# Scaling the attention probabilities of three groups of heads on ScalarE instead of VectorE, in a four-layer single-core kernel

## The chip, the cores and the metric

The kernel is one program on one core of a Trainium2 chip. Its engines are TensorE (PE in the profile), VectorE (DVE), ScalarE (ACT), GpSimd (POOL, idle here) and SyncE (SP, which issues the DMAs). The metric is the device time of one execution in microseconds (us). Every engine works through its own instructions in order; a wait at the head of an engine's queue holds all that is behind it.

## The reference

Two kinds of layer, two layers of each, on 256 tokens of width 1024. The first kind is not touched. The second kind projects its input to four attention mixers of four heads each, and the change is in the softmax of three of them:

```
def forgetting_attention(q, k, v, log_f):            # mixer b
    ...
    logits = einsum('bthd,bshd->bhts', qb, k) * scale
    logits = where(causal, logits + decay, NEG_INF)
    probs = softmax(logits, axis=-1)
    return einsum('bhts,bshd->bthd', probs, v)
# dsa_attention (mixer a): the same with the keys cut to the top-k of an index score
# sliding_window_sink_attention (mixer d): the same with a window, and a sink in the sum
# differential_attention (mixer c): probs[:, 0] - lam * probs[:, 1], of 8 maps
x = x + rmsnorm(mix @ w_out); m = square(relu(h @ w_up)) @ w_down; ...
```

## The kernel before

All matmuls are on TensorE, most of them with operands split into a rounded high part and a remainder, three matmuls for one product. A weight panel goes by DMA into a ring of 8 slots; ScalarE writes its rounded part (`round_weights`, L2575) and VectorE the remainder (`subtract_rounded`, L2757, signal `panels_subtracted`) before TensorE may use it.

A layer of the second kind begins with the mixers. Each engine has there an order written out by hand, the table `ORDER`: a list of words such as `in` (one projection), `panel` (one weight panel), `c`, `b`, `a`, `d` (one step of that mixer). Each engine's part of a mixer is a generator (`attend`, `attend_d`), and each word runs it to its next `yield`. The mixers come in the order c, b, a, d. The 256 queries of a mixer are two tiles, t=0 (128 keys) and t=1 (256 keys). For mixer i and tile t the steps are:

- TensorE `scores`: the logits into PSUM banks (`name_sc..`).
- VectorE `masked_scores` (L2819, L2823, L2828): scale, mask and move them to the buffer `Ls[i % 2]`, row maxima, signal `score_max`.
- ScalarE `exps` (L2587): one exponential for each head with the negative maximum as bias and the row sum as second output (`den`), signal `exps`.
- VectorE `probs`: reciprocal of the sums (L2843), one multiplication of all heads by it (L2845: 128x512 for t=0, 128x1024 for t=1), signal `probs`. For c two more instructions (L2849) subtract the second map.
- TensorE `turned` (L2240): transposes of the probabilities; ScalarE `turned_rows_of` moves them out of PSUM (`drain_bank`, L2579, written to `all_rest`), signal `PT`; TensorE `values`.

After its values, mixer c has a norm: ScalarE copies `c_o` out of PSUM and squares it (L2652, signal `o_sq`), TensorE sums the squares (`c_ss`, a 128x512 product behind the wait on `o_sq`), ScalarE makes the reciprocal root (L2656, L2658), VectorE applies it (L2950). In ScalarE's order this copy and square stand right behind the exponentials of b, t=1. The parts `early`, `rest` and `late` on TensorE are the output projection `mix`; `early` waits until VectorE has split the results of c and b (L2763, L2765, signal `mix_split`).

The name `all_work` in the profile holds the buffers of scores, q, k and v and many others, `all_rest` the transposed probabilities, `all_ring` the weight panels. Numbers of lines in both files differ by a few.

Of the kernel before, what the change touches and what calls it, by code (L numbers as in the profile page):

```python
# [11 lines left out]
ALU = mybir.AluOpType  # L12
ACT = mybir.ActivationFunctionType
# [4 lines left out]
NT = T // P  # L18
# [100 lines left out]
class Signals:  # L119
# [11 lines left out]
    def due(self, layer, name, n):  # L131
        return self.sem[name], self.base[name] + layer * self.per_layer[name] + n
# [82 lines left out]
class Memory:  # L215
# [9 lines left out]
    def area(self, name):  # L225
        return Area(self.plain[name][:, :], self.parts[name])
# [64 lines left out]
def turns_in(order, steps, size=lambda step: 1):  # L291

    at = {key: [i for i, x in enumerate(order) if x == name][step] for key, (name, step) in steps.items()}
    return {key: sum(size(other) for other in at if at[other] <= at[key]) for key in at}
# [400 lines left out]
def params2(a):  # L695
# [27 lines left out]
    return out  # L723

SIGNALS2 = {
    "raw": 9, "copied": 6, "roped": 9, "probs": 8, "PT": 12, "o_sq": 1, "nlf": 1, "mix_split": 5, "gT": 16, "p_split": 1, "score_max": 8, "exps": 8,
    "gate_abs": 9, "gate_ln": 1, "relu_used": 6, "relu": 6, "c_oT": 1, "o_rstd": 1, "lam_sum": 1, "lam_exp": 1, "pT_in": 1, "ff_relu": 16,
    "ff_squared": 16, "g_hi": 16, "gates": 4, "cosined": 9, "proj_out": 4, "o_copied": 2,
}


# [1385 lines left out]
def block2(nc, ctx, kit, banks, ring_all, A, earlier):  # L2117

    rounded, hT, mixT, x = kit.rounded, kit.hT, kit.mixT, kit.x
    S = Signals(nc, ctx, SIGNALS2, earlier)  # L2120
# [4 lines left out]
    def psum_of(layer):  # L2125
        return banks.of(f"2{layer}")

    def ring_of(layer):
        return ring_all.of(f"2{layer}")

    def due_in(layer):
        return lambda name, n: S.due(layer, name, n)
# [22 lines left out]
    lam = buf(80)  # L2155
# [9 lines left out]
    raw, turned = area(2, 2, T), area(2, 2, T)  # L2165
    LN = 8 * P * 3
    Ls = [area(LN), area(LN)]
# [11 lines left out]
    gates, proj, yn = area(4, 512), area(4, 512), area(4, 512)  # L2179

    def scores_of(buffer, t, maps):

        n = P * (t + 1)
        lo = maps * P * t
        return buffer[:, lo:lo + maps * n].rearrange("p (e n) -> p e n", n=n)
# [19 lines left out]
    ATTENDED = [("c", 8, 32 ** -0.5, 4), ("b", 4, HD ** -0.5, 2), ("a", 4, HD ** -0.5, 0), ("d", 4, HD ** -0.5, 6)]  # L2205
# [16 lines left out]
            a:3 split:2 d in d:2 panel d early p early d a early rest early d:2 rest late rest late d rest"""),  # L2222
    }
    MIXERS = [(name, t) for name, *_ in ATTENDED for t in range(NT)]
    maxima, probabilities, exponentials = (turns_in(ORDER[engine], {(name, t): (name, first + t) for name, t in MIXERS})
                                           for engine, first in (("DVE", 0), ("DVE", 2), ("ACT", 1)))
    turned_rows = turns_in(ORDER["ACT"], {(name, t): (name, 3 if name == "d" and not t else 4 + t) for name, t in MIXERS}, lambda step: step[1] + 1)
    copied_out = turns_in(ORDER["ACT"], {"b": ("b", 6), "a": ("a", 6)})
    split_off = turns_in(ORDER["DVE"], {"c": ("split", 0), "b": ("split", 1), "a": ("split", 2), "d0": ("d", 5), "d1": ("d", 7)})
# [4 lines left out]
    def tensor(pe, layer, following):  # L2234

        psum, ring, due = psum_of(layer), ring_of(layer), due_in(layer)
        mm, mm3, used = kit.mm, kit.mm3, kit.used

        def transpose(out, a):
            return nc.tensor.transpose(out, a, kit.ident)  # L2240
# [110 lines left out]
        def turned(i, t):  # L2351

            name, maps, _, _ = ATTENDED[i]
            pe.wait_ge(*due("probs", probabilities[name, t]))
            for kt in range(t + 1):
                b = psum.claim(pe, f"{name}_pt{t}{kt}")
                for e in range(4):
                    m = e if maps == 4 else 4 * (e // 2) + e % 2
                    last = transpose(b[:, e * P:(e + 1) * P], scores_of(Ls[i % 2], t, maps)[:, m, kt * P:(kt + 1) * P])
                last.then_inc(psum.full_of(f"{name}_pt{t}{kt}"), 1)  # L2360
# [199 lines left out]
    def stat_of(i, t, what, n):  # L2560

        lo = 16 + 48 * (i % 2) + 8 * t + {"neg": 0, "den": 16, "rec": 32, "sink": 36}[what]
        return stat[:, lo:lo + n]

    def scalar(act, layer):

        psum, ring, due = psum_of(layer), ring_of(layer), due_in(layer)
        A_ = nc.scalar.activation
# [8 lines left out]
        def drain_bank(name, out, signal, rows=slice(0, P), part=slice(0, 512)):  # L2577
            act.wait_ge(*psum.filled(name))
            A_(out, psum.bank(name)[rows, part], ACT.Copy).then_inc(*psum.freed(name))  # L2579
            act.drain().then_inc(S[signal], 1)  # L2580

        def exps(i, t):
            name, maps, _, _ = ATTENDED[i]
            act.wait_ge(*due("score_max", maxima[name, t]))
            L = scores_of(Ls[i % 2], t, maps)
            for e in range(maps):
                A_(L[:, e, :], L[:, e, :], ACT.Exp, bias=stat_of(i, t, "neg", maps)[:, e:e + 1],  # L2587
                   accum_out=stat_of(i, t, "den", maps)[:, e:e + 1])
            if name == "d":
                A_(stat_of(i, t, "sink", 4), stat_of(i, t, "sink", 4), ACT.Exp)  # L2590
            act.drain().then_inc(S["exps"], 1)

        def project():

            yield
            for name, panel, kind, parts in IN_USES:
                if name in ROPED_AT:
                    i = ROPED_AT[name]
                    tiles = ROPED[i][3]
                    if i >= 2:  # L2600
                        act.wait_ge(*due("roped", i - 1))
                    drain_bank(name, raw[:, i % 2, 0:tiles, :], "raw", part=slice(0, tiles * T))
                elif name in ("b_q", "b_k"):
                    drain_bank(name, qk[name], "copied")
                elif name in vtok:
                    drain_bank(name, vtok[name], "copied", part=slice(0, NT * parts[1]))
                yield
            yield
# [24 lines left out]
        def turned_rows_of(i, t):  # L2633
            name = ATTENDED[i][0]
            if i >= 2 and not t:
                act.wait_ge(*psum.filled(ATTENDED[i - 2][0] + "_o"))
            for kt in range(t + 1):
                drain_bank(f"{name}_pt{t}{kt}", PTs[i % 2][:, kt, :, t * P:(t + 1) * P], "PT")

        def attend(i):  # L2640
            name = ATTENDED[i][0]
            yield
            for t in range(NT):
                exps(i, t)
                yield
            yield
            for t in range(NT):
                turned_rows_of(i, t)
                yield
            if name == "c":  # L2650
                drain_bank("c_o", oT, "c_oT")
                A_(osq, oT, ACT.Square).then_inc(S["o_sq"], 1)  # L2652
                yield
                kit.exp_and_ln()
                act.wait_ge(*psum.filled("c_ss"))
                A_(ors, shaped(psum.bank("c_ss"), 2, T), ACT.Ln, bias=kit.eps, scale=1.0 / HD).then_inc(*psum.freed("c_ss"))  # L2656
                act.drain()
                A_(ors, ors, ACT.Exp, scale=-0.5).then_inc(S["o_rstd"], 1)  # L2658
                yield
                yield  # L2660
            else:
                drain_bank(name + "_o", qk[name + "_q"], "o_copied")
                yield
            yield

        def attend_d():
            yield
            for t in range(NT):
                exps(3, t)
                yield  # L2670
            turned_rows_of(3, 0)
            yield
            yield
            turned_rows_of(3, 1)
            yield
            yield
            yield
# [69 lines left out]
    def vector(dve, layer):  # L2747

        psum, ring, due = psum_of(layer), ring_of(layer), due_in(layer)
        PAR = par_of(layer)  # L2750
        V = nc.vector
# [82 lines left out]
        def probs(i, t):  # L2834
            name, maps, _, _ = ATTENDED[i]
            n = P * (t + 1)
            L = scores_of(Ls[i % 2], t, maps)
            den, rec = stat_of(i, t, "den", maps), stat_of(i, t, "rec", maps)
            dve.wait_ge(*due("exps", exponentials[name, t]))
            if name == "d":  # L2840
                V.tensor_tensor(den, den, stat_of(i, t, "sink", 4), ALU.add)
                dve.drain()
            V.reciprocal(rec, den)  # L2843
            dve.drain()
            V.tensor_tensor(L, L, rec.unsqueeze(2).broadcast_to([P, maps, n]), ALU.mult)  # L2845
            if name == "c":
                dve.drain()
                for g in range(2):
                    V.scalar_tensor_tensor(L[:, 4 * g:4 * g + 2, :], L[:, 4 * g + 2:4 * g + 4, :], lam[:, 68:69],  # L2849
                                           L[:, 4 * g:4 * g + 2, :], ALU.mult, ALU.add)  # L2850
            dve.drain().then_inc(S["probs"], 1)

        def select(t):
# [407 lines left out]
```

## Time and profile before

| | |
|---|---|
| median of 3 runs | 1681.28 us (1680.44 to 1684.38) |
| profiled execution, its own time | 1682.12 us |
| its span | 1680.3 us |
| mean granted TensorE clock | 0.977 of full |
| PE busy | 1594.1 us (95%) |
| DVE busy | 1093.7 us (65%) |
| ACT busy | 767.5 us (46%) |

The profile is of one execution. The two layers of the second kind take the last half of the span; their mixer parts lie around 900 to 1055 us and 1320 to 1450 us. Busy shares are means over parts with different limits; what matters for an edit in the mixers is which wait ends last there.

### The profile page before, as it was taken

To read this page: it belongs to the slowest core of one execution; us is meant where nothing else is said; L and a number is where in the kernel's file an instruction comes from. 1 tells how busy PE (TensorE), PEld (TensorE's weight loads), DVE (VectorE), ACT (ScalarE), POOL (GpSimd) and SP (SyncE) were. 2 spreads that over 40 slices of the span, in tenths; PEclk is the share of its full clock that TensorE was granted. 3 is DMA by queue.
4 is the path that set the end of the run, shared out by engine and by line. 5 is a ranking of instruction groups with operands and counts; after the bars stand their busy time and mean duration, and the time that the engine had idled before them with its cause. 6 is when DMAs were issued, how large, how long until landed. Compare 5 with 4: busy or idle time off the path is not lost.

```text
span 1680.3 us, 29569 instructions
## 1 busy us (share of the span) xinstructions
PE 1594.1 (95%) x12124; PEld 1425.4 (85%) x12124; DVE 1093.7 (65%) x1609; ACT 767.5 (46%) x1151; POOL 0.2 (0%) x4
## 2 busy tenths in 40 slices
PE   7999989999999989899999989999999979999998
PEld 7987569998898856799989877899889978799887
DVE  2865666776466666577854897666353798766545
ACT  3524254444345332544443355655344446655434
POOL 0000000000000000000000000000000000000000
PEclk9999899999999989899999999999999989999999
DMA  7421024655642200366554432456554433355552
GB/s 249 145 87 52 1 80 138 193 175 201 198 138 69 77 26 1 125 216 199 190 201 121 122 80 92 159 176 201 190 197 134 127 92 109 103 189 198 186 190 100
DMA packets 186310, 232.23 MB, mean 138 GB/s; under 512 B 22560, under 2 KB 161600, under 8 KB 186048
## 3 DMA queue, kind: packets, MB, share of 16 engines
q1 hardware_dynamic: 186176, 230.34, 42.5%
q8 instruction: 96, 1.57, 0.4%
q14 instruction: 38, 0.31, 0.1%
HBM read 229.28 MB, written 1.05 MB: 137 GB/s over the span
## 4 chain that ended last, share of the span: by engine, by line
PE 83%; DVE 10%; DVEq 3%; issue 2%; ACT 2%; DMA 1%; ACTq 0%; SPq 0%
PE banks L432 82%; DVE all_ring_rounded L2757 2%; DVE all_rest L2926 1%; DVE all_work L2861 1%; DMA all_ring<-in_w_ple_gate 1%; DVEq L2860 1%; DVE x_state L381 0%; DVE all_work L2823 0%; PE banks L2240 0%; DVEq L384 0%; DVE all_work L2819 0%; DVE all_work L2845 0%; ACT all_rest L2579 0%; DVEq L2821 0%; PE banks L927 0%
## 5 line engine op out<-in xcount | busy, mean ns | idle before, releaser
L432 PE MATMUL banks<-all_mix_rounded,all_ring_rounded 128*128 128x256 f32 (+2 forms) x3584 | 666.7, 287 | 17.0 <-DVEq L428 7.5
L432 PEld LDWEIGHTS banks<-all_mix_rounded,all_ring_rounded 128*128 128x128 f32 (+2 forms) x3584 | 566.5, 193 | 26.6 <-DVEq L428 8.7
L432 PE MATMUL banks<-all_work_rounded,all_ring_rounded 128*128 128x256 f32 x1792 | 511.1, 285 | 0.0
L432 PE MATMUL banks<-all_ring_rounded,all_work_rounded 128*128 128x512 f32 (+1 forms) x1856 | 462.4, 377 | 3.2 <-DVE all_ring_rounded L2757 1.7
L432 PEld LDWEIGHTS banks<-all_ring_rounded,all_work_rounded 128*128 128x128 f32 x1856 | 347.0, 188 | 69.6 <-issue 2.7
L432 PEld LDWEIGHTS banks<-all_work_rounded,all_ring_rounded 128*128 128x128 f32 x1792 | 346.1, 193 | 1.8 <-issue 1.4
L2757 DVE TENSOR_TENSOR all_ring_rounded<-all_ring,all_ring_rounded 128x2048 fp32r<-128x2048 f32 x104 | 237.6, 2291 | 149.6 <-ACT all_ring_rounded L2575 146.8
L1609 DVE TENSOR_TENSOR all_ring_rounded<-all_ring,all_ring_rounded 128x2048 fp32r<-128x2048 f32 (+2 forms) x96 | 213.6, 2232 | 83.3 <-ACT all_ring_rounded L1366 80.8
L2575 ACT ACTIVATE all_ring_rounded<-all_ring 128x2048 fp32r<-128x2048 f32 x104 | 198.2, 1910 | 118.9 <-DMA all_ring<-in_w_mlp_down 87.1
L1366 ACT ACTIVATE all_ring_rounded<-all_ring 128x2048 fp32r<-128x2048 f32 (+2 forms) x96 | 177.7, 1858 | 112.4 <-DMA all_ring<-in_w_in 54.3
L432 PE MATMUL banks<-all_work 64*64 64x64 f32 (+10 forms) x2084 | 172.9, 272 | 18.5 <-ACTq L1541 6.0
L432 PEld LDWEIGHTS banks<-all_work 64*64 64x64 f32 (+4 forms) x2084 | 124.3, 153 | 47.6 <-issue 24.8
L432 PE MATMUL banks<-all_ring_rounded,all_mix_rounded 128*128 128x256 f32 (+2 forms) x640 | 143.7, 307 | 3.3 <-DVE all_ring_rounded L2757 2.3
L432 PEld LDWEIGHTS banks<-all_ring_rounded,all_mix_rounded 128*128 128x128 f32 x640 | 103.8, 191 | 11.9 <-DVE all_ring_rounded L2757 2.8
L432 PE MATMUL banks<-all_work,all_ring 128*128 128x128 f32 x704 | 101.7, 289 | 1.9 <-issue 1.9
L432 PEld LDWEIGHTS banks<-all_work,all_ring 128*128 128x128 f32 x704 | 87.9, 195 | 3.0 <-issue 3.0
L1583 ACT ACTIVATE all_work<-all_work 128x256 f32<-128x256 f32 x44 | 18.4, 418 | 125.3 <-DVE all_work L2017 125.3
L1370 ACT ACTIVATE all_work<-banks 128x512 f32<-128x512 f32 (+2 forms) x74 | 37.1, 502 | 81.9 <-PE banks L432 65.8
L432 PEld LDWEIGHTS banks<-all_rest,all_work 128*64 128x64 f32 (+2 forms) x504 | 48.4, 164 | 22.7 <-issue 9.0
L432 PE MATMUL banks<-all_rest,all_work 128*128 128x128 f32 (+5 forms) x504 | 60.6, 289 | 6.9 <-ACTq L2580 5.0
L432 PE MATMUL banks<-all_work,all_rest 128*64 128x256 f32 (+7 forms) x292 | 58.6, 379 | 2.4 <-ACT all_work L1377 2.1
L2715 ACT ACTIVATE all_work<-banks 128x512 f32<-128x512 f32 x32 | 19.1, 597 | 81.8 <-PE banks L432 81.8
(258 smaller groups left out, 1252.8 us busy)
## 6 DMA issues: line engine op xcount, KB each, us to landing
all_ring<-in_w_in SPq DMA_DIRECT2D x48, 1024.0 KB, 5.4
all_ring<-in_w_mlp_up SPq DMA_DIRECT2D x32, 1024.0 KB, 5.4
all_ring<-in_w_mlp_down SPq DMA_DIRECT2D x32, 1024.0 KB, 4.9
all_ring<-in_ffn_w_gate SPq DMA_DIRECT2D x22, 1024.0 KB, 5.3
all_ring<-in_ffn_w_up SPq DMA_DIRECT2D x22, 1024.0 KB, 5.5
all_ring<-in_ffn_w_down SPq DMA_DIRECT2D x22, 1024.0 KB, 4.9
all_ring<-in_w_out SPq DMA_DIRECT2D x16, 512.0 KB, 4.3
all_ring<-in_w_out SPq DMA_DIRECT2D x8, 1024.0 KB, 5.0
```

Of the source, the lines that this page charges most:

```text
L432: ins = self.nc.tensor.matmul(out, lhsT, rhs, start=start, stop=stop)
L1366: A_(rounded(ring.view(name + "_hi")), raw, ACT.Copy).then_inc(ring_all.rounded, 1)
L1370: A_(out, psum.bank(name)[rows, part], func, scale=scale).then_inc(*psum.freed(name))
L1583: A_(gcv[:, j % 2, 2, :], gcv[:, j % 2, 1, :], ACT.Gelu_apprx_tanh).then_inc(S["ff_gelu"], 1)
L1609: V.tensor_tensor(rounded(ring.view(name)), ring.view(name), as_float32(rounded(ring.view(name + "_hi"))), ALU.subtract).then_inc(ring_all ...
L2575: A_(rounded(ring.view(name + "_hi")), raw, ACT.Copy).then_inc(ring_all.rounded, 1)
L2715: A_(gh[:, 2 * c:2 * c + 2, :], shaped(psum.bank(f"ff{c}"), 2, T), ACT.Relu).then_inc(*psum.freed(f"ff{c}"))
L2757: V.tensor_tensor(rounded(ring.view(name)), ring.view(name), as_float32(rounded(ring.view(name + "_hi"))), ALU.subtract).then_inc(ring_all ...
L2860: dve.drain()
L2861: V.max(best, acc[t])
L2926: last = V.scalar_tensor_tensor(acc[t], r, weight, acc[t], ALU.mult, ALU.add)
```

## The change

For b, a and d VectorE's `probs` stops after the reciprocal and raises a new signal, `inverted`. ScalarE gets a new function, `scale_probs`: it waits for `inverted` and multiplies each head's scores, with a Copy activation whose scale is the column of reciprocals, in four instructions of 128x128 (t=0) or 128x256 (t=1), then raises `scaled`, for which TensorE's transposes now wait. Mixer c is as before. `scale_probs(i, 0)` runs in the same step as the exponentials of t=1, `scale_probs(i, 1)` in the next step; `ORDER` is not changed.

```
         def turned(i, t):
...
-            pe.wait_ge(*due("probs", probabilities[name, t]))
+            pe.wait_ge(*(due("probs", t + 1) if name == "c" else due("scaled", scaled[name, t])))
...
+        def scale_probs(i, t):
+            name, maps, _, _ = ATTENDED[i]
+            act.wait_ge(*due("inverted", inverted[name, t]))
+            L = scores_of(Ls[i % 2], t, maps)
+            for e in range(maps):
+                A_(L[:, e, :], L[:, e, :], ACT.Copy, scale=stat_of(i, t, "rec", maps)[:, e:e + 1])
+            act.drain().then_inc(S["scaled"], 1)
...
             for t in range(NT):
                 exps(i, t)
-                yield
+                if t and name != "c":
+                    scale_probs(i, 0)
+                yield
+            if name != "c":
+                scale_probs(i, 1)
             yield
...
         def attend_d():
             yield
-            for t in range(NT):
-                exps(3, t)
-                yield
+            exps(3, 0)
+            yield
+            exps(3, 1)
+            scale_probs(3, 0)
+            yield
+            scale_probs(3, 1)
             turned_rows_of(3, 0)
...
             V.reciprocal(rec, den)
+            if name != "c":
+                dve.drain().then_inc(S["inverted"], 1)
+                return
             dve.drain()
             V.tensor_tensor(L, L, rec.unsqueeze(2).broadcast_to([P, maps, n]), ALU.mult)
```

Three places of the order show what moves. The first is ScalarE in the first layer of the second kind, from the exponentials of b, t=1 on (`bank2` is the projection b_v, `bank0` is `c_o`, and the line after them is the square). Before:

```order
L2587 ACTIVATE all_work<-all_work 128x256 [waits score_max]
L2587 ACTIVATE all_work<-all_work 128x256 x3
L2579 ACTIVATE all_work<-banks 128x512 [waits bank2_filled]
L2579 ACTIVATE all_work<-banks 128x512 [waits bank0_filled]
L2652 ACTIVATE all_work<-all_work 128x512
L2575 ACTIVATE all_ring_rounded<-all_ring 128x2048 [waits slot3_freed,slot2_filled]
L2579 ACTIVATE all_work<-banks 128x512 [waits bank1_filled]
L322 ACT_TABLE_LOAD
```

And of the change, at the same place:

```order
L2590 ACTIVATE all_work<-all_work 128x256 [waits score_max]
L2590 ACTIVATE all_work<-all_work 128x256 x3
L2601 ACTIVATE all_work<-all_work 128x128 [waits inverted]
L2601 ACTIVATE all_work<-all_work 128x128 x3
L2582 ACTIVATE all_work<-banks 128x512 [waits bank2_filled]
L2582 ACTIVATE all_work<-banks 128x512 [waits bank0_filled]
L2667 ACTIVATE all_work<-all_work 128x512
L2578 ACTIVATE all_ring_rounded<-all_ring 128x2048 [waits slot3_freed,slot2_filled]
L2582 ACTIVATE all_work<-banks 128x512 [waits bank1_filled]
L2601 ACTIVATE all_work<-all_work 128x256 [waits inverted]
L2601 ACTIVATE all_work<-all_work 128x256 x3
L322 ACT_TABLE_LOAD
```

The two copies and the square of c now stand behind four instructions that wait for VectorE. The second place is VectorE at the reciprocals that this waits for, those of b. Before:

```order
L2757 TENSOR_TENSOR all_ring_rounded<-all_ring,all_ring_rounded 128x2048 [waits panels_rounded] x2
L2843 RECIPROCAL all_work<-all_work 128x4 [waits exps]
L2845 TENSOR_TENSOR all_work<-all_work 128x512
L2843 RECIPROCAL all_work<-all_work 128x4 [waits exps]
L2845 TENSOR_TENSOR all_work<-all_work 128x1024
L2950 SCALAR_TENSOR_TENSOR all_work<-all_work 128x512 [waits o_rstd]
```

And of the change:

```order
L2775 TENSOR_TENSOR all_ring_rounded<-all_ring,all_ring_rounded 128x2048 [waits panels_rounded] x2
L2861 RECIPROCAL all_work<-all_work 128x4 [waits exps] x2
L2970 SCALAR_TENSOR_TENSOR all_work<-all_work 128x512 [waits o_rstd]
L2972 TENSOR_SCALAR all_work<-all_work 128x512
L2837 SCALAR_TENSOR_TENSOR all_work<-banks,all_rest 128x256 [waits bank4_filled,bank7_filled]
```

The reciprocals of b keep their place behind two panels; the two multiplications are gone. The third place is ScalarE at mixer a, between its exponentials and the copies of its transposed probabilities (`all_rest`). Before:

```order
L2587 ACTIVATE all_work<-all_work 128x256 [waits score_max]
L2587 ACTIVATE all_work<-all_work 128x256 x3
L2575 ACTIVATE all_ring_rounded<-all_ring 128x2048 [waits slot7_freed,slot6_filled]
L2579 ACTIVATE all_work<-banks 128x256 [waits bank6_filled]
L2579 ACTIVATE all_rest<-banks 128x4x128 [waits bank1_filled,bank0_filled]
```

And of the change:

```order
L2590 ACTIVATE all_work<-all_work 128x256 [waits score_max]
L2590 ACTIVATE all_work<-all_work 128x256 x3
L2601 ACTIVATE all_work<-all_work 128x128 [waits inverted]
L2601 ACTIVATE all_work<-all_work 128x128 x3
L2578 ACTIVATE all_ring_rounded<-all_ring 128x2048 [waits slot7_freed,slot6_filled]
L2582 ACTIVATE all_work<-banks 128x256 [waits bank6_filled]
L2601 ACTIVATE all_work<-all_work 128x256 [waits inverted]
L2601 ACTIVATE all_work<-all_work 128x256 x3
L2582 ACTIVATE all_rest<-banks 128x4x128 [waits bank1_filled,bank0_filled]
```

Eight instructions are added between the exponentials and the first of these copies; TensorE's transposes of a, t=1 wait for the last four of them.

## Rows read from the trace of the kernel before

**Rows 1.** The page: span, and the chain that ended last, by engine.
```profile
span 1680.3 us, 29569 instructions
...
PE 83%; DVE 10%; DVEq 3%; issue 2%; ACT 2%; DMA 1%; ACTq 0%; SPq 0%
```

**Rows 2.** Waits of PE in the whole span: total us, times, longest.
```profile
PE banks L2240 <- DVEq L2851: 9.0, 2, 4.5
```

**Rows 3.** Timeline of ACT, first layer: start us, us, what; [idle before].
```profile
1003.08 1.31 ACT L2579 ACTIVATE all_work<-banks 128x512 f32<-128x512 f32 x2
1004.50 0.63 ACT L2652 ACTIVATE all_work<-all_work 128x512 f32<-128x512 f32 x1
```

**Rows 4.** Timeline of DVE, the same place.
```profile
1003.25 4.50 DVE L2757 TENSOR_TENSOR all_ring_rounded<-all_ring,all_ring_rounded 128x2048 fp32r<-128x2048 f32 x2
1007.66 0.17 DVE L2843 RECIPROCAL all_work<-all_work 128x4 f32<-128x4 f32 x1
```

**Rows 5.** Timeline of PE, the sums `c_ss` in the first layer.
```profile
1007.01 1.02 PE L432 MATMUL banks<-all_work 128*128 128x512 f32 x2
```

**Rows 6.** Timelines of ACT, DVE and PE: the same place, second layer.
```profile
1397.67 0.63 ACT L2652 ACTIVATE all_work<-all_work 128x512 f32<-128x512 f32 x1
...
1400.87 0.17 DVE L2843 RECIPROCAL all_work<-all_work 128x4 f32<-128x4 f32 x1
...
1400.08 1.02 PE L432 MATMUL banks<-all_work 128*128 128x512 f32 x2
```

**Rows 7.** Groups by line and form, whole span: busy us, mean ns | idle before.
```profile
L2845 DVE TENSOR_TENSOR all_work<-all_work 128x512 f32<-128x512 f32 x6 | 4.2, 693 | 0.8 <-issue 0.4
L2845 DVE TENSOR_TENSOR all_work<-all_work 128x1024 f32<-128x1024 f32 x8 | 9.8, 1226 | 0.6
...
L2587 ACT ACTIVATE all_work<-all_work 128x128 f32<-128x128 f32 x40 | 15.6, 390 | 40.6 <-DVEq L2832 40.3
L2587 ACT ACTIVATE all_work<-all_work 128x256 f32<-128x256 f32 x40 | 19.8, 496 | 0.2
```

**Rows 8.** Timeline of ACT: copies with a column as scale, second layer.
```profile
1462.49 1.14 ACT L359 ACTIVATE all_work<-banks,all_work 128x128 f32<-128x128 f32 x4 [0.25 <-PE banks L432]
```

**Rows 9.** Timeline of PE at mixer c, first layer: a wait for probabilities.
```profile
982.06 0.79 PE L2240 MATMUL banks<-all_rest,all_work 128*128 128x128 f32 x4 [4.50 <-DVEq L2851]
```

**Rows 10.** Stretches: us, busy (x) of PE, PEld, DVE, ACT, POOL; PEclk, DMA share, GB/s.
```profile
961.00:965.00 4.00, 3.50 (x16) 3.53 (x17) 3.71 (x9) 1.03 (x5) 0.00 (x0) 0.50 0.43 109
962.00:963.00 1.00, 1.00 (x7) 1.00 (x6) 0.91 (x3) 0.00 (x0) 0.00 (x0) 0.50 0.08 16
966.00:967.00 1.00, 1.00 (x11) 1.00 (x10) 0.91 (x2) 1.00 (x7) 0.00 (x0) 1.00 0.72 242
982.00:989.00 7.00, 6.94 (x35) 6.94 (x35) 6.55 (x8) 0.60 (x1) 0.00 (x0) 0.53 0.01 2
```

**Rows 11.** Timeline of ACT, mixer a, first layer.
```profile
1027.03 1.92 ACT L2575 ACTIVATE all_ring_rounded<-all_ring 128x2048 fp32r<-128x2048 f32 x1 [0.15 <-issue]
1028.85 0.36 ACT L2579 ACTIVATE all_work<-banks 128x256 f32<-128x256 f32 x1
1030.64 2.02 ACT L2579 ACTIVATE all_rest<-banks 128x512 f32<-128x512 f32 x3 [1.42 <-PE banks L2240]
```

**Rows 12.** Timeline of DVE, mixer a, first layer.
```profile
1028.15 0.18 DVE L2843 RECIPROCAL all_work<-all_work 128x4 f32<-128x4 f32 x1
```

**Rows 13.** Timeline of PE, mixer a and the start of the output projection, first layer.
```profile
1029.48 1.94 PE L2240 MATMUL banks<-all_rest,all_work 128*128 128x128 f32 x16 [0.38 <-issue]
...
1032.74 2.22 PE L432 MATMUL banks<-all_rest,all_work 128*64 128x256 f32 x16 [1.33 <-ACTq L2580]
...
1036.33 0.72 PE L432 MATMUL banks<-all_ring_rounded,all_work_rounded 128*128 128x512 f32 x2 [0.71 <-DVEq L2778]
```

**Rows 14.** Timelines of ACT and PE, mixer d, t=0, first layer.
```profile
1045.89 0.19 ACT L2590 ACTIVATE all_work<-all_work 128x4 f32<-128x4 f32 x1
...
1045.93 0.60 PE L2240 MATMUL banks<-all_rest,all_work 128*128 128x128 f32 x4
```

More of the change, by code:

```diff
@@ L725 @@
 SIGNALS2 = {
-    "raw": 9, "copied": 6, "roped": 9, "probs": 8, "PT": 12, "o_sq": 1, "nlf": 1, "mix_split": 5, "gT": 16, "p_split": 1, "score_max": 8, "exps": 8,
+    "raw": 9, "copied": 6, "roped": 9, "probs": 2, "PT": 12, "o_sq": 1, "nlf": 1, "mix_split": 5, "gT": 16, "p_split": 1, "score_max": 8, "exps": 8,
     "gate_abs": 9, "gate_ln": 1, "relu_used": 6, "relu": 6, "c_oT": 1, "o_rstd": 1, "lam_sum": 1, "lam_exp": 1, "pT_in": 1, "ff_relu": 16,
-    "ff_squared": 16, "g_hi": 16, "gates": 4, "cosined": 9, "proj_out": 4, "o_copied": 2,
+    "ff_squared": 16, "g_hi": 16, "gates": 4, "cosined": 9, "proj_out": 4, "inverted": 6, "scaled": 6, "o_copied": 2,
 }
@@ L2224, in block2 @@
     MIXERS = [(name, t) for name, *_ in ATTENDED for t in range(NT)]
-    maxima, probabilities, exponentials = (turns_in(ORDER[engine], {(name, t): (name, first + t) for name, t in MIXERS})
-                                           for engine, first in (("DVE", 0), ("DVE", 2), ("ACT", 1)))
+    maxima, exponentials = (turns_in(ORDER[engine], {(name, t): (name, first + t) for name, t in MIXERS})
+                            for engine, first in (("DVE", 0), ("ACT", 1)))
+    PLAIN = [(name, t) for name, t in MIXERS if name != "c"]
+    inverted = turns_in(ORDER["DVE"], {(name, t): (name, 2 + t) for name, t in PLAIN})
+    scaled = turns_in(ORDER["ACT"], {(name, t): (name, 2 + t) for name, t in PLAIN})
     turned_rows = turns_in(ORDER["ACT"], {(name, t): (name, 3 if name == "d" and not t else 4 + t) for name, t in MIXERS}, lambda step: step[1] + 1)
@@ L2843, in probs @@
             V.reciprocal(rec, den)
+            if name != "c":
+                dve.drain().then_inc(S["inverted"], 1)
+                return
             dve.drain()
             V.tensor_tensor(L, L, rec.unsqueeze(2).broadcast_to([P, maps, n]), ALU.mult)
[L2846 to L2850, printed above, removed]
+            dve.drain()
+            for g in range(2):
+                V.scalar_tensor_tensor(L[:, 4 * g:4 * g + 2, :], L[:, 4 * g + 2:4 * g + 4, :], lam[:, 68:69],
+                                       L[:, 4 * g:4 * g + 2, :], ALU.mult, ALU.add)
             dve.drain().then_inc(S["probs"], 1)
```

## The prediction, on record before the changed kernel ran

> **What bounds the kernel now.** I read the page first: TensorE makes 83% of the chain that ended last, VectorE 10%, ScalarE 2% [rows 1]. So an edit on the other two engines counts only where TensorE waits for them, and VectorE's 65% of busy time says nothing yet. The waits of TensorE came second. The one wait for probabilities in them, 9.0 us in two times, is for L2851, the end of `probs` [rows 2]; the timeline puts it at mixer c [rows 9], which the change leaves alone, and nothing that the change removes stands ahead of it in VectorE's order. Third, I followed the timelines of the three engines through b, a and d and asked at each multiplication who waits for it, and at each place where ScalarE gets new work who waits for what stands behind it.
>
> **What is removed.** Per layer VectorE loses three multiplications of 128x512 (0.69 us) and three of 128x1024 (1.23 us) [rows 7]: 3 x 1.92 = 5.8 us. TensorE never waited for these. All that the freed time can reach is the wait of 0.71 us ahead of `early`, for the split of b's result [rows 13].
>
> **What is added.** Per layer ScalarE gets 12 copies of 128x128 and 12 of 128x256 with a column as scale. The nearest row is the same instruction out of PSUM: four of 128x128 take 1.14 us [rows 8]. The exponential, which reads the same buffer and also gives a sum, takes 0.39 us a piece [rows 7], 1.56 for four; these are the bounds, and I take 1.2 as nearer to the copy. For 128x256 the exponential is 0.11 us longer (0.50 against 0.39), so four copies are 1.14 + 0.42 = 1.56 to 4 x 0.50 = 2.0; I take 1.65. Together 3 x 2.85 = 8.6 us on ScalarE for 5.8 on VectorE, and one more hop for each probability: reciprocal, signal, ScalarE. The Trainium skill, "ScalarE: Activation LUTs", section "Rules for kernel authors", says to use VectorE and not ScalarE for a multiplication. The times above agree with it, but by that alone the change would cost nothing wherever ScalarE has idle time. What costs is the order.
>
> **First place: ScalarE waits for b's reciprocal.** Before, ScalarE was through with the exponentials of b and began to copy b_v and `c_o` at 1003.08, and the square of c began at 1004.50 and ended at 1005.13 [rows 3]. VectorE is then at 1003.25 with two panels, 4.50 us, and makes the first reciprocal of b at 1007.66 to 1007.83 [rows 4]. Before nobody cared. Now `scale_probs(b, 0)` is ahead of the copies, so ScalarE stands from 1003.0 to 1007.9, scales until 1009.1 and starts the copies at 1009.2, 6.1 us late. TensorE had reached the sums `c_ss`, which need the square, at 1007.01 without a wait [rows 5], that is 1.9 us after the square ended. So TensorE now stands for 6.1 - 1.9 = 4.2 us, and all matmuls behind it in its order with it. In the second layer the square ends at 1398.30, its copies began 1.42 us ahead of it, at 1396.25, the reciprocal is at 1400.87 to 1401.04 and `c_ss` at 1400.08 [rows 6]: the copies start at 1401.1 + 1.2 + 0.1 = 1402.4, 6.15 us late, minus 1.8 is 4.35. I take 4.3 us for each layer. The scaling of b, t=1 (1.65 us) and the late norm of c lie beside the projection d_q, which TensorE works on for 6 us, and cost nothing more; without that cover they would add up to 1.65.
>
> **The clock after the stall.** A wait of TensorE of 4.50 us at 982.06 [rows 9] was followed by 7 us at a granted clock of 0.53, nearly all at the lower level (1.2 GHz) [rows 10]. After a shorter one, dense matmuls ran at 0.50 through 961 to 965 and at 1.00 by 966; 7 matmuls were done in a microsecond at the one level and 11 at the other [rows 10]. A stall of 4.3 us is next to the first of these, and d_q behind it is dense like the second. At half clock for 4 us the loss is 4 x (1 - 7/11) = 1.45 us, for 7 us 2.5. I take 1.8, and 0 and 2.5 as ends. The Trainium skill, "TensorE: Matmul & The Clock Gate", section "HAM oscillation — how this bites in real kernels", says that a wait that lets the clock drop is paid a second time by the ramp after it. The trace agrees, with the 0.53 just named.
>
> **Second place: mixer a.** By then all engines are late by the same 6.1 us, since ScalarE and VectorE both wait for TensorE at the scores of a; I go on in the old times. ScalarE ends the exponentials of a, t=1 at 1026.9, rounds a panel at 1027.03, copies d_v at 1028.85 for 0.36 us, and begins the three copies of transposed rows at 1030.64, after 1.42 us of idle time [rows 11]. Now it scales t=0 until 1028.1 (its reciprocal comes long before), rounds until 1030.2, copies until 1030.5, and scales t=1, whose reciprocal was there at 1028.3 [rows 12], until 1032.25. TensorE has done the transposes of p and of a, t=0 by 1030.4 [rows 13] and waits for the rest. ScalarE's three copies, 2.02 us, then end at 1034.3 in place of 1032.66, and TensorE's values of a start at 1034.4 in place of 1032.74 [rows 13]: 1.65 us late. Of this 0.7 comes back: the wait of 0.71 ahead of `early` goes, for VectorE, rid of two multiplications, splits b about 0.8 earlier. Net 1.0 us.
>
> **Third place: mixer d.** ScalarE ended the exponentials of d, t=1 at 1046.08, and TensorE was at the transposes of d, t=0 at 1045.93 without a wait [rows 14]. Now those need `scale_probs(d, 0)`, which stands behind the exponentials of t=1: 1046.1 + 1.2 = 1047.3, and 0.15 for the signal and for ScalarE's own lag. Cost 1.5 to 1.6 us. The scaling of d, t=1 ends some 1.7 us later and the copy 0.7 after that, under the 12 matmuls of 128x512 that TensorE has there.
>
> **Sum.** 4.3 + 1.8 + 1.0 + 1.6 = 8.7 us for a layer, 17.4 for two. Nothing behind gives it back: the rest of such a layer is dense TensorE work. Against the profiled execution (1682.1 us, span 1680.3) that is 1699.5; the median of the runs lies 0.8 below that execution, so 1698.7 us.
>
> **The rivals.** A change of over 0.3%, 5 us, can be told from none here.
> (1) The same, dearer in clock: the two waits at a come close together (1.8 and 1.1 us), and the clock may drop there too, for 1.5 to 2.5 us, and the first loss be 2.5. Then 11 to 13 us a layer, 1703 to 1707. Against it: the 1.33 and 0.71 us of waiting at the same place did not drop it so far. 0.18.
> (2) The stall without the clock: 6.9 us a layer or, if the later two places are half absorbed, 5 to 6; 1691 to 1695. For it: the place where the clock falls is not fixed to a wait's end. 0.12.
> (3) No change: ScalarE's wait is hidden. For that VectorE would have to make b's reciprocal before 1003.7 (the 1.9 us of slack less 1.2 of scaling), and two panels of 2.25 us stand ahead of it. Only if both were passed early; 0.05. 1677 to 1686.
> (4) Faster: the 5.8 us taken off VectorE pull the chain in. It decides where TensorE waits for VectorE behind b: 0.71 us a layer [rows 13], and as much again if panel remainders come earlier, so 1678 to 1680 at best, if the first place costs nothing. The 10% of VectorE in the chain speaks for it; that these lie ahead of the change's first instruction speaks against. 0.03.
> The forecast itself, 12 to 22 us more, has 0.62.
>
> **The range.** The low end takes in (2), the high end most of (1), with the bounds of the copies (0.3 us at each of three places and two layers, 2 us) in both: 1690 to 1706. Slower by over 0.3%: 0.92; within: 0.05; faster: 0.03.
>
> **What would show it.** In the new profile: a wait of ScalarE of about 4.8 us for VectorE's reciprocal ahead of the first scaling of b, in both layers; a wait of TensorE of about 4.3 us ahead of `c_ss`, for ScalarE's square; a granted clock of 0.5 for 4 to 7 us behind it; transposes of a in two parts with waits of 1 to 2 us; a wait of 1.5 us ahead of d's first transposes. Four scalings should take 1.2 and 1.65 us. I am wrong if the square is there in time, or if TensorE's idle time grows by less than 5 us a layer.

## The result, and the profile after

The changed kernel takes 1708.84 us (median of 4 runs, 1704.46 to 1708.98) against 1680.86 us before (4 runs). The ratio is 1.0154, with a 95% interval of 1.0138 to 1.0169: slower by 1.5%. The ratio is not the quotient of the two medians, which lie 28.0 us apart; by the ratio the loss is 25.9 us. The profiled execution is the run of 1704.46 us. Ratios are of undisturbed executions, so one of the ten of the kernel b_late below, 1968.44 us at a mean clock of 0.746, is left out.

The page gives the span and, again, the chain that ended last by engine. TensorE's share fell from 83% [rows 1] to 77%; the shares of VectorE and ScalarE rose.

```profile
span 1702.5 us, 29605 instructions
...
PE 77%; DVE 12%; DVEq 4%; ACT 3%; issue 2%; DMA 1%; ACTq 0%; SPq 0%
```

The waits of TensorE from 900 us on (engine, line <- whom: us in total, times, longest):

```profile
PE banks L2243 <- DVEq L2871: 9.0, 2, 4.5
PE banks L432 <- ACT all_work L2667: 8.4, 2, 4.7
PE banks L2243 <- ACTq L2602: 6.8, 4, 2.0
```

The first is c's old wait, the same as in [rows 2]. The other two are new: 8.4 us for c's square (L2667), 6.8 us for scaled probabilities (L2602, the end of `scale_probs`). They are the three places of the prediction. I take the first of them first, in the timelines of ScalarE, VectorE and TensorE (start us, us, what, [idle before]):

```profile
1006.82 1.28 ACT L2601 ACTIVATE all_work<-all_work 128x128 f32<-128x128 f32 x4 [4.44 <-DVEq L2863]
1008.20 1.31 ACT L2582 ACTIVATE all_work<-banks 128x512 f32<-128x512 f32 x2
1009.62 0.63 ACT L2667 ACTIVATE all_work<-all_work 128x512 f32<-128x512 f32 x1
...
1002.17 4.50 DVE L2775 TENSOR_TENSOR all_ring_rounded<-all_ring,all_ring_rounded 128x2048 fp32r<-128x2048 f32 x2
1006.59 0.47 DVE L2861 RECIPROCAL all_work<-all_work 128x4 f32<-128x4 f32 x2
...
1010.30 2.08 PE L432 MATMUL banks<-all_work 128*128 128x512 f32 x2 [3.73 <-ACT all_work L2667]
```

ScalarE stands 4.44 us until VectorE is through two panels and has made the reciprocal, then scales, then copies and squares. TensorE stands 3.73 us ahead of `c_ss`, 4.71 in the second layer, and `c_ss` itself takes 2.08 us in place of 1.02 [rows 5]. Second place, mixer a, ScalarE and TensorE:

```profile
1036.78 1.71 ACT L2601 ACTIVATE all_work<-all_work 128x256 f32<-128x256 f32 x4
1038.64 2.02 ACT L2582 ACTIVATE all_rest<-banks 128x512 f32<-128x512 f32 x3 [0.15 <-issue]
...
1038.56 1.09 PE L2243 MATMUL banks<-all_rest,all_work 128*128 128x128 f32 x8 [1.95 <-ACTq L2602]
1040.75 3.53 PE L432 MATMUL banks<-all_rest,all_work 128*64 128x256 f32 x16 [1.09 <-ACTq L2583]
...
1442.45 1.62 PE L2243 MATMUL banks<-all_rest,all_work 128*128 128x128 f32 x8 [1.96 <-ACTq L2602]
1444.79 4.16 PE L432 MATMUL banks<-all_rest,all_work 128*64 128x256 f32 x16 [0.72 <-ACTq L2583]
```

The transposes are cut in two by a wait of 1.95 us, and a's values wait 1.09 more. The values then take 3.53 and, in the second layer, 4.16 us, against 2.22 [rows 13]. Third place, mixer d: eight scalings in a row on ScalarE, and TensorE waits 1.47 us for the first four:

```profile
1054.72 3.08 ACT L2601 ACTIVATE all_work<-all_work 128x128 f32<-128x128 f32 x8
...
1056.08 0.66 PE L2243 MATMUL banks<-all_rest,all_work 128*128 128x128 f32 x4 [1.47 <-ACTq L2602]
```

Last the granted clock, in stretches (us, busy (x) of PE, PEld, DVE, ACT, POOL; PEclk, DMA share, GB/s):

```profile
1010.00:1016.00 6.00, 5.70 (x20) 4.67 (x21) 0.00 (x0) 5.79 (x9) 0.00 (x0) 0.50 0.33 107
...
1040.00:1043.00 3.00, 2.25 (x10) 1.59 (x12) 1.28 (x4) 0.60 (x1) 0.00 (x0) 0.51 0.01 2
...
1000.00:1070.00 70.00, 61.19 (x388) 50.50 (x387) 37.80 (x62) 44.46 (x102) 0.00 (x0) 0.93 0.27 91
```

Half clock follows the first place for 6 us and the second for 3. Over 1000 to 1070 the mean is 0.93; over the same work the kernel before had 1.00:

```profile
1000.00:1060.00 60.00, 57.39 (x397) 48.26 (x394) 44.55 (x70) 36.48 (x78) 0.00 (x0) 1.00 0.31 106
```

Measured between starts on TensorE that both traces have (c's values, b's values, a's values, d's last values), the layers compare with the forecast so. The starts before are 999.02, 1017.16, 1032.74, 1056.43 and after 998.42, 1023.24, 1040.75, 1066.62; in the second layer 1392.08, 1410.23, 1425.81, 1449.51 and 1402.42, 1427.12, 1444.79, 1471.65.

| stretch | forecast, us | first layer | second layer |
|---|---|---|---|
| c's values to b's (first place, its clock) | 6.1 | +6.7 | +6.6 |
| b's values to a's (second place) | 1.65 | +1.9 | +2.1 |
| a's values to d's last (0.7 back, 1.6 at d) | 0.9 | +2.2 | +3.2 |
| sum | 8.7 | +10.8 | +11.8 |

The two layers together give 22.6 us; the span grew by 22.2 (1702.5 - 1680.3). Waits of TensorE make 13.0 us of it: 3.73 and 4.71 ahead of `c_ss`, 1.0 and 0.6 more than before around a, 1.47 and 1.45 at d; the forecast had 13.8. What is left goes with the half clock: 4.8 us in the stretch of the first place (2.95 and 1.84; the forecast had 3.6), and 4.8 in the other two stretches, where the forecast had nothing.

### The profile page after: what moved, and what is told of

The parts are those of the page before. It is cut to its first block, busy times and chain, and to the rows that moved or that the text cites. A ratio compares the mean times of both kernels' runs of the same rounds, so it can differ in the third digit from the quotient of the medians.

```text
span 1702.5 us, 29605 instructions
## 1 busy us (share of the span) xinstructions
PE 1602.2 (94%) x12124; PEld 1427.5 (84%) x12124; DVE 1082.1 (64%) x1597; ACT 784.9 (46%) x1199; POOL 0.2 (0%) x4
## 4 chain that ended last, share of the span: by engine, by line
PE 77%; DVE 12%; DVEq 4%; ACT 3%; issue 2%; DMA 1%; ACTq 0%; SPq 0%
PE banks L432 76%; DVE all_ring_rounded L2775 2%; DVE all_work L2841 1%; ACT all_work L2590 1%; DVE all_ring_rounded L1609 1%; DVE all_rest L2946 1%; DVE all_work L2881 1%; DMA all_ring<-in_w_ple_gate 1%; DVE all_work L2837 1%; ACT all_ring_rounded L2578 1%; DVEq L2880 1%; DVEq L2839 0%; DVE x_state L381 0%; DVE all_work L2866 0%; DVEq L384 0%
## 5 line engine op out<-in xcount | busy, mean ns | idle before, releaser
L432 PEld LDWEIGHTS banks<-all_rest,all_work 128*64 128x64 f32 (+2 forms) x504 | 50.8, 170 | 24.0 <-issue 10.9
L432 PE MATMUL banks<-all_rest,all_work 128*128 128x128 f32 (+5 forms) x504 | 64.5, 302 | 6.1 <-ACTq L2583 4.2
```

What stands on the lines that cost most here:

```text
L432: ins = self.nc.tensor.matmul(out, lhsT, rhs, start=start, stop=stop)
```

## The experiments

Two theories were put against each other. **Queue**: what costs is what stands behind the new waits and scalings in ScalarE's order, at three places, and the clock after them. **Work**: what costs is the amount of new work on ScalarE. All comparisons are with the kernel before on the same chip, and a price in us is what the ratio makes of its median there, unless medians are named.

**One mixer at a time.** The edit is the same in the three; mixers that are not in `ON` are multiplied on VectorE as before:

```
+    ON = ("b",)                       # then ("a",), then ("d",)
...
-            if name != "c":
+            if name in ON:
                 dve.drain().then_inc(S["inverted"], 1)
                 return
```

*b_only.*

> Only mixer b is scaled on ScalarE; a and d are multiplied on VectorE as before. Queue theory (the copies and the square of c stand behind a wait for b's reciprocal): this holds the whole first place, 4.3 us of TensorE stall a layer and 1.5 to 3 us of half clock behind it, so 12 to 15 us more than before, 1693 to 1696, and the stall ahead of c_ss is there in full. Work theory (what costs is the 8.6 us a layer of new ScalarE work): a third of the whole loss of 24 to 28, so 8 to 9 us, 1689 to 1690.

Measured: 1694.86 us, ratio 1.0076 (1.0061 to 1.0091), that is 12.8 us. The waits of TensorE from 900 us on, and the new instruction on ScalarE by its line:

```profile
PE banks L432 <- ACT all_work L2669: 9.2, 2, 4.6
```

```profile
L2603 ACT ACTIVATE all_work<-all_work x16: 385/447/511, 1007.9 to 1414.0; 128x128 f32<-128x128 f32 x8, 128x256 f32<-128x256 f32 x8
its engine sat idle before it (us, times) until:
  DVEq L2863: 9.9, 2
```

The stall is there in full, 4.6 us a layer, and the time is the queue theory's.

*a_only.*

> Only mixer a is scaled on ScalarE. Queue theory: no wait for VectorE stands ahead of c's square, so c_ss is on time; what is left is the second scaling of a ahead of the copies of its transposed rows, 1.0 us a layer, and up to 1.5 us a layer if the clock drops there: 2 to 5 us more than before, 1683 to 1686. Work theory: a third of the loss, 8 to 9 us, 1689 to 1690.

Measured: 1689.64 us, ratio 1.0043 (1.0029 to 1.0058), 7.2 us. This is over the queue theory's 2 to 5 and just under the work theory's 8 to 9. It told nothing apart, and it showed that a's price had been set too low.

*d_only.*

> Only mixer d is scaled on ScalarE. Queue theory: TensorE waits 1.5 us a layer ahead of d's first transposes, without a fall of the clock: 3 us more than before, 1684. Work theory: 8 to 9 us, 1689 to 1690.

Measured: 1685.73 us, ratio 1.0021 (1.0011 to 1.0030), 3.5 us, as the queue theory has it. TensorE's waits at d are 2.9 us of it, in two. The three losses, 0.76%, 0.43% and 0.21%, add to 1.40%; the whole change in the same comparison, below, has 1.48% (1.31 to 1.65). So within the interval the prices of the places add up, and they differ by a factor of 3.6 where the new work is the same: amounts of work don't explain them.

**The change once more**, unedited, for a second trace.

> The changed kernel once more, for a second trace: its runs lay at 1704.5 and at 1708.7 to 1709.0, and the trace seen is of the first. If the clock makes the difference, TensorE's waits are the same in both traces to some tenths of a us, and only the stretches at half clock are longer or more, by some 8 us in all. If a wait makes it, one wait of TensorE is some 2 us longer in each layer.

Measured: 1706.88 us (1703.59 to 1707.84), ratio 1.0148 (1.0131 to 1.0165), 24.9 us. Its profiled execution was again its shortest run, so the longer ones were not seen in a trace. But the two traces differ in the way in question. TensorE's waits in this one, from 900 us on:

```profile
PE banks L432 <- ACT all_work L2667: 8.2, 2, 4.3
PE banks L2243 <- ACTq L2602: 6.7, 4, 1.9
```

and a stretch of 70 us over the same work as above:

```profile
997.00:1067.00 70.00, 60.78 (x387) 49.74 (x383) 37.10 (x62) 43.42 (x101) 0.00 (x0) 0.90 0.27 91
```

These sums of waits agree to 0.2 us, though single waits ahead of `c_ss` do not (4.28 and 3.96 here, 3.73 and 4.71 there); the clock is 0.90 there, where the other trace has 0.93. So the time at half clock differs between two executions whose waits at these places come to the same. The difference of some 8 us that was expected for the longer runs can't be seen in a trace of the shortest, and stays open.

**The wait without the scaling.** The kernel before, with one wait and its signal added:

```
             for t in range(NT):
                 exps(i, t)
+                if t and name == "b":
+                    act.wait_ge(*due("inverted", 1))
```

> The kernel before, with one thing added: behind the exponentials of b, t=1, ScalarE waits for the reciprocal of b, t=0. No scaling is moved. Queue theory: ScalarE is held until 1007.9 as in the change, only the 1.2 us of scaling are missing, so TensorE stalls 3.1 us a layer ahead of c_ss and loses 1.5 to 3 us at half clock: 9 to 12 us more than before, 1691 to 1694. Work theory: no work is added, so no change.

Measured: 1693.07 us, ratio 1.0061 (1.0044 to 1.0079), 10.3 us. ScalarE's timeline and TensorE's wait:

```profile
1008.68 1.31 ACT L2584 ACTIVATE all_work<-banks 128x512 f32<-128x512 f32 x2 [4.95 <-DVEq L2863]
1010.11 0.63 ACT L2669 ACTIVATE all_work<-all_work 128x512 f32<-128x512 f32 x1
```

```profile
PE banks L432 <- ACT all_work L2669: 6.1, 2, 3.2
```

A wait that adds no work costs most of what b costs (10.3 us, interval 7.4 to 13.3, of 12.8). The stall is 3.2 and 2.8 us, the forecast 3.1.

**The scaling without the wait.** The kernel before, with four copies on a spare buffer at the same place. They change nothing of what is computed:

```
+                if t and name == "b":
+                    for e in range(4):
+                        part = kit.junk[:, e * P:(e + 1) * P]
+                        A_(part, part, ACT.Copy, scale=C("ones")[:, 0:1])
+                    act.drain()
```

> The kernel before, with four copies of 128x128 with a column as scale added at the same place in ScalarE's order, on a spare buffer and without any wait for VectorE. The multiplications stay on VectorE. Queue theory: c's square is 1.2 us later, within its 1.9 us of slack, so nothing changes (within 2 us of before). Work theory: some 1.2 us a layer, 2.4 in all. The four copies also give the price: 1.2 us expected.

Measured: 1682.98 us, ratio 1.0007 (0.9996 to 1.0017): nothing that can be told. The copies took 0.39 us a piece:

```profile
L2661 ACT ACTIVATE all_rest<-all_rest,all_work x8: 387/389/406, 1004.0 to 1398.1; 128x128 f32<-128x128 f32 x8
```

With the run before it this closes the first place: the work costs nothing where it stands alone, and the wait costs most of the price alone. Behind the wait the scaling does count, for it then lies in the stall: 9.2 us ahead of `c_ss` in b_only, 6.1 with the wait alone.

**b, scaled a step later.** Only b on ScalarE, both tiles behind c's square:

```
             for t in range(NT):
                 exps(i, t)
-                if t and name in ON:
-                    scale_probs(i, 0)
                 yield
             if name in ON:
+                scale_probs(i, 0)
                 scale_probs(i, 1)
```

> Only mixer b is scaled on ScalarE, and both of its tiles in the step of t=1, behind the copies and the square of c. Queue theory: all of b's work stays on ScalarE, but c's square is on time again, b's scaled rows are there 3 us before TensorE wants them, and nothing is lost: within 2 us of before, against 12.8 more with the t=0 scaling one step earlier. Work theory: as much as b alone cost, 8 to 13 us.

Measured: 1683.63 us, ratio 1.0011 (1.0001 to 1.0021), 1.9 us (0.2 to 3.5) against 12.8. ScalarE and TensorE:

```profile
1004.43 0.63 ACT L2669 ACTIVATE all_work<-all_work 128x512 f32<-128x512 f32 x1
...
1008.91 3.09 ACT L2604 ACTIVATE all_work<-all_work 128x128 f32<-128x128 f32 x8
...
1006.78 1.02 PE L432 MATMUL banks<-all_work 128*128 128x512 f32 x2
...
1017.49 2.22 PE L432 MATMUL banks<-all_rest,all_work 128*64 128x256 f32 x16 [0.76 <-ACTq L2586]
```

The square is on time, `c_ss` doesn't wait, and the eight scalings, all of the work moved for b, lie beside TensorE's projection. Only the wait ahead of b's values is longer, 0.76 us and 0.83 in the second layer against 0.20 before. The work theory is out.

**The whole change with that edit.**

> The whole change, with the scaling of t=0 of b and a moved to the step of t=1 (d as in the change). Queue theory: b's loss of 12.8 us goes; a keeps its loss, since the scaling still stands ahead of the copies of its transposed rows, and so does d: 7.2 + 3.5 = 10 to 11 us more than before, 1692 to 1694. Work theory: the same as the change, 24 to 27 more.

Measured: 1693.88 us, ratio 1.0071 (1.0054 to 1.0088), 11.9 us; the sum of a and d alone was 10.7. Of the change's loss of 24.9 to 25.9 us, 13 to 14, more than half, go with one step of order.

**Is a's price the clock?** Only a on ScalarE, a second time, and a twin in which TensorE works through its waits at a: two matmuls of 128x512 on constants ahead of the wait for a's scaled rows, one ahead of the wait for its copies. They write banks that are overwritten behind them. The edit ahead of the scaled rows (the one ahead of the copies is of the same form):

```
+            if name == "a" and t:
+                ahead = psum.claim(pe, "a_pt10")
+                for _ in range(2):
+                    mm(ahead[:, :], C("heads64"), rope.rearrange("p a b n -> p (a b n)")[:, 0:512])
             pe.wait_ge(*(due("scaled", scaled[name, t]) if name in ON else due("probs", probabilities[name, t])))
...
```

> Only mixer a is scaled on ScalarE, once more, beside its filled twin: 7 us more than before (1.004), as measured.

> As the kernel with only a on ScalarE, and TensorE does matmuls of 128x512 on constants in its two waits at a (two ahead of the transposes of a, t=1, one ahead of a's values), about as long as the waits, into banks that are overwritten behind them. Clock theory (a's loss beyond 1 us a layer is the clock, which falls because TensorE has little to do around those waits): the values of a take 2.2 us again in place of 3.7 to 4.1, and the loss shrinks from 7 us to 1 to 3 us, 1682 to 1685. If the loss is in the waits or in something behind them: 7 us or more, since the matmuls can only add.

Measured: 1690.48 us, ratio 1.0040 (1.0027 to 1.0053), and with the matmuls 1685.80 us, ratio 1.0014 (1.0004 to 1.0024). TensorE is given three more matmuls a layer, and the kernel is 4.7 us faster by the medians. The values of a and the stretch around them, unfilled:

```profile
1035.71 4.17 PE L432 MATMUL banks<-all_rest,all_work 128*64 128x256 f32 x16 [0.80 <-ACTq L2585]
```

```profile
1000.00:1065.00 65.00, 61.63 (x402) 51.01 (x403) 43.96 (x70) 40.85 (x87) 0.00 (x0) 0.95 0.30 98
```

and filled:

```profile
1032.92 2.22 PE L432 MATMUL banks<-all_rest,all_work 128*64 128x256 f32 x16 [0.23 <-ACTq L2596]
```

```profile
1000.00:1065.00 65.00, 63.14 (x409) 51.38 (x408) 46.35 (x71) 42.69 (x92) 0.00 (x0) 1.00 0.32 107
```

So a costs 2.4 us by its waits (1.2 a layer; the forecast was 1.0) and 4 to 5 by the clock, which the forecast's sum had at nothing. The traces say the same. From the start of c's values to d's first transposes TensorE took 46.91 and 46.95 us in the two layers before, 50.52 and 50.79 with a on ScalarE, and 48.07 and 48.34 with its waits filled: 2.45 us in each layer are the clock's, 1.2 and 1.4 are the waits'.

**Where VectorE's time would be worth something.** TensorE's one large wait for VectorE is at c, and ahead of c's reciprocals VectorE works 9.8 us on the second selection of the top keys, which only a's masks need. VectorE in the kernel before:

```profile
969.30 0.42 DVE L2858 TENSOR_TENSOR all_rest<-all_rest,all_work 128x256 f32<-128x256 f32 x1 [0.17 <-issue]
...
978.68 0.43 DVE L2867 TENSOR_TENSOR all_rest<-all_rest,all_work 128x256 f32<-128x256 f32 x1
...
979.51 0.20 DVE L2843 RECIPROCAL all_work<-all_work 128x8 f32<-128x8 f32 x1
```

The kernel before, with VectorE's order changed, and then the same with b scaled as in b_late:

```
-  ... index panel in panel c:2 select forget:2 c:2 panel
-      forget in b in c panel b c in c panel c in panel b:2 c a c b:2 ...
+  ... index panel in panel c:4 forget:2 panel
+      forget in b in c panel b c in c panel c in panel b:2 select c a c b:2 ...
```

> The kernel before (all multiplications on VectorE) with VectorE's order changed: the second selection of the top keys, 9.8 us, which only the masks of a need, moves from ahead of c's probabilities to behind the reciprocals and multiplications of b. If the one wait of TensorE for probabilities (4.5 us a layer at c, with 7 us at half clock behind it) is what VectorE costs, it goes: 4.5 us and 2 to 3 us of clock a layer, less what VectorE is late by at the masks of a, 1 to 2 us: 8 to 12 us faster than before, 1669 to 1674.

Measured: 1679.71 us, ratio 0.9981 (0.9971 to 0.9990): 3.2 us, where 8 to 12 were expected. The wait at c is gone, and c's values start at 989.72 in place of 999.02, but two others have come, from 900 us on:

```profile
PE banks L432 <- DVE all_work L2837: 9.8, 4, 2.8
PE banks L2245 <- DVEq L2872: 3.4, 2, 2.4
```

The first is for masked scores: c's 5.6 us, as in the other kernels, and 4.2 more at a, for whose masks VectorE is now late by more than the 1 to 2 us expected. The second is for a's probabilities. The clock falls there again in the first layer, where a's values take 3.82 us; in the second, behind waits of 0.96 and 1.00 us, they take 2.22. Part of the gain was given back a mixer later.

> The same order, and b scaled on ScalarE in the step of t=1 (which cost nothing by itself). VectorE is now the tighter engine between b and a, so its 1.9 us a layer less of multiplication should show: 0 to 3 us faster than the reordered kernel alone. If VectorE is not the limit there, the same time as it.

Measured: 1673.01 us, ratio 0.9937 (0.9922 to 0.9952). The same scaling that cost 1.9 us (0.2 to 3.5) in the old order now gains 6.7 us by the medians, over twice the most expected:

```profile
PE banks L432 <- DVE all_work L2837: 5.6, 2, 2.8
PE banks L2246 <- DVEq L2872: 3.5, 2, 1.9
```

The 4.2 us of waiting at a's masks are gone. This version beats both kernels, by 0.6% and by about 2%. By its trace, a's values still start at half clock in both layers (4.16 us each), so it is not at its end; that was not tried.

## Why the prediction was wrong in its size

The direction and the three places held. The order of their prices did not: the sum had a (1.0 us a layer) below d (1.6), and alone a costs 7.2 us in two layers and d 3.5. The median lies 2.8 us above the range, the profiled execution inside it. By its own steps:

- *Removed: nothing that TensorE waits for.* Right: c's wait is still 9.0 us in two. In the changed order of VectorE it would have been wrong: there b's scaling on ScalarE gained 6.7 us.
- *Price of a scaling, 1.2 and 1.65 us for four.* 1.28 and 1.71 measured.
- *First place, a stall of 4.3 us.* 3.73 and 4.71; the run with the wait alone shows the cause.
- *The clock after it, 1.8 us.* 2.95 and 1.84, so undersized by 0.6 us a layer; the first lies above the end of 2.5 that was given. The stretch, stall and clock together, is 0.5 us longer than forecast.
- *Second place, net 1.0 us.* The waits were sized rightly, 1.95 and 1.09 us against 1.85 and 1.1. **This is the step that failed**: its sum gave the clock nothing and left that to rival (1), at 0.18, because waits of 1.33 and 0.71 us had not dropped it before. It dropped in every trace in which a was scaled on ScalarE and the waits were not filled. The filled run measures it: 4 to 5 us in two layers, and the traces of the change and of a alone give 4.8 and 4.9. That is nearly the whole of the 5.2 us by which the layers exceed the sum (22.6 against 17.4); the clock at the first place is 1.2 more, and the waits, smaller than forecast, take 0.8 back. The mechanism of rival (1) is what happened. Its terms, 1.5 to 2.5 us at a and 2.5 at the first place, add up to 10.9 to 11.9 us a layer and not to the 13 that it names, and 10.8 and 11.8 were measured; the median of 1708.84 us lies above its 1703 to 1707 too.
- *Third place, 1.6 us.* 1.47 of wait; d alone costs 3.5 us in two layers. The clock did not fall behind this wait: d's first transposes took 0.66 us and the granted clock was 1.00 over 1054 to 1060 us. Why it fell behind the two waits at a and not behind this one was not tested.
- *The step from the profiled execution to the median.* The sum gave 1699.5 us for such an execution, and it took 1704.46; the median was then taken as 0.8 lower, and it is 4.4 higher. That is half of the miss of 10.1 us, and no rows stood behind it but one execution and three runs. The longer runs have a lower mean clock, 0.969 to 0.970 against 0.972. At that span 0.002 is 7 us more at half clock; by the 7 and 11 matmuls a microsecond of [rows 10] that is an estimate of 2.5 us. Another part can lie ahead of the change: in the twelve traces in which all work before it is the same, c's values of the first layer start between 995.66 and 1000.05 us. How the 4.4 divide stays open, since none of the longer runs was traced.

The prediction also argued that a stall that drops the clock is paid a second time. The Trainium skill, "TensorE: Matmul & The Clock Gate", section "A second HAM failure mode: psum-queue depth-cycling", tells of another case: in one kernel, short but frequent pauses between groups of matmuls made the clock go up and down. The trace of this kernel agrees at place a, where no wait was over 1.96 us and the clock was 0.51.

## What to carry to other kernels

When work moves to an engine with idle time, read what stands behind it in that engine's order and when the new wait will end: the wait, not the amount of work, set the price here, and one step later the same work cost 1.9 us in place of 12.8. Relief for an engine is worth something only where another waits for it; scaling b on ScalarE cost 13 us, cost 2 or gained 7, by the order around it. Each new pause of TensorE, a short one too, needs a term for the clock in the sum, or a trace that says it is nothing: it was 2.45 us a layer at a and nothing at d. And the one profiled execution can lie several us from the median: 4.4 and 3.3 us below it in the two traces of the change, 3.0 below in the kernel with filled waits, so a range for the median needs room for it.

## What the hardware showed

A Copy with a column as scale, 128x128 from SBUF, took 0.385 us at the least (the row of the kernel with b alone), and so did an exponential with bias and sum over the same buffer (0.390 in the mean, [rows 7]). But four such copies in a row took 1.28 us, so one starts each 0.30 us, while the exponentials, each followed by the read of its sum, started 0.39 us apart. Four copies of each size in a row took 3.08 us.

The time at half clock differs between executions in a part that the edit doesn't touch. Over the first 840 us, the layers of the first kind, before and after:

```profile
0.00:840.00 840.00, 792.60 (x6699) 701.54 (x6700) 553.98 (x901) 352.05 (x532) 0.20 (x4) 0.97 0.40 128
```

```profile
0.00:840.00 840.00, 790.45 (x6703) 697.15 (x6704) 553.97 (x901) 352.67 (x532) 0.20 (x4) 0.98 0.40 128
```

The count of half-clock time is not a count of lost time: with the higher clock of the second line, c's values started only 0.6 us earlier (998.42 against 999.02).

And filling TensorE's waits with work that is thrown away made the kernel 0.26% faster than its twin: the three matmuls cost less than the clock that they kept.
